# Router product of a two-layer flow backbone: the weights become the stationary operand, in two column tiles, and a second product turns the result back

## The reference, cut to what matters

```python
h2 = modulate(x, sh2, sc2)                       # (tokens, 1024)
f = hier_moe(h2.reshape(-1, d), w_router_group[layer], w_router_expert[layer], ...)

def hier_moe(t, w_router_group, w_router_expert, ...):
    p_group = jax.nn.softmax((t @ w_router_group).astype(jnp.float32), axis=-1)   # 4 groups
    grp = jnp.argmax(p_group, axis=-1).astype(jnp.int32)
    logits_e = jnp.einsum('td,dge->tge', t, w_router_expert)                      # 4 x 8 experts
    logits_sel = jnp.take_along_axis(logits_e, grp[:, None, None], axis=1)[:, 0]
    top_p, top_j = lax.top_k(jax.nn.softmax(logits_sel, axis=-1), TOP_K_FINE)     # 2 of 8
    ...
    return grouped_experts(...)
```

## Time and profile before

| | us |
|---|---|
| median of 3 runs | 2699.07 |
| the profiled execution | 2698.96 |
| its span, first to last instruction | 2697.1 |
| PE busy in it | 2331.0 (86%) |
| `attend` of layer 0, first scores to last logits | 376.6 to 684.2 |
| `attend` of layer 1, first scores to last logits | 1664.2 to 1916.0 |
| mean granted TensorE clock | 0.927 of full |

### The profile page before, as it was taken

How to read it: one execution, slowest core, us unless ns; L and a number is a source line. 1 busy time by engine, 2 the same in 40 slices (tenths; PEclk the granted TensorE clock), 3 DMA queues, 4 the chain that set the end, 5 groups by cost and what they waited for, 6 DMA issues and landing times. The chain is left out here.

```text
span 2697.1 us, 39484 instructions
## 1 busy us (share of the span) xinstructions
PE 2331.0 (86%) x15320; PEld 1642.8 (61%) x15320; DVE 863.8 (32%) x2138; ACT 430.6 (16%) x1058; POOL 500.2 (19%) x629
## 2 busy tenths in 40 slices
PE   4999879998299999999949987999389999999950
PEld 3999745654266666666629984556266666666630
DVE  1322435564610111101127665565711011111008
ACT  1010122221011111111101113222001111111112
POOL 0000013444011111111110011344011111111117
PEclk8999979998599999999979998999589999999985
DMA  9454430001397999999841113000289999999943
GB/s 356 147 185 153 155 109 11 22 22 41 136 369 294 392 400 389 387 399 394 327 160 65 47 41 130 20 24 16 83 349 391 391 384 395 386 386 381 371 190 128
DMA packets 130505, 608.65 MB, mean 226 GB/s; under 512 B 20608, under 2 KB 23680, under 8 KB 111984
## 3 DMA queue, kind: packets, MB, share of 16 engines
q1 hardware_dynamic: 112400, 569.61, 54.5%
q0 software_dynamic: 16864, 37.78, 3.7%
q10 hardware_dynamic: 1152, 0.03, 0.0%
HBM read 599.41 MB, written 42.04 MB: 238 GB/s over the span
## 5 line engine op out<-in xcount | busy, mean ns | idle before, releaser
L1874 PEld LDWEIGHTS gate_up<-room,w_gate_up 128*128 128x128 f32 x4608 | 521.1, 193 | 31.5 <-issue 31.5
L1874 PE MATMUL gate_up<-room,w_gate_up 128*128 128x128 f32 x4608 | 528.0, 277 | 3.1 <-DVE room L1781 3.1
L1883 PE MATMUL down<-w_down,room 128*128 128x512 f32 x576 | 256.8, 599 | 0.0
L1891 PE MATMUL gate_up_short<-w_gate_up,room 128*64 128x512 f32 x1152 | 255.1, 595 | 0.0
L1790 DVE TENSOR_TENSOR room<-room,gate_up 128x128 f32<-128x128 f32 x144 | 41.4, 288 | 597.8 <-ACT room L1809 597.8
L1891 PEld LDWEIGHTS gate_up_short<-w_gate_up,room 128*64 128x64 f32 x1152 | 79.5, 137 | 171.2 <-issue 171.2
L1883 PEld LDWEIGHTS down<-w_down,room 128*128 128x128 f32 x576 | 106.5, 190 | 123.0 <-issue 120.5
L1793 DVE TENSOR_TENSOR room<-room,gate_up_short 128x256 f32<-128x256 f32 x36 | 15.2, 421 | 495.1 <-ACT room L1815 495.1
L1501 POOL COPY rows_idx<-slot_token 128x1 int32 (+1 forms) x78 | 14.3, 183 | 789.9 <-PE rows_turned L1861 709.2
L1904 PE MATMUL down<-w_down,room 128*64 128x512 f32 x576 | 131.5, 598 | 11.9 <-ACT room L1817 11.9
L1325 PE MATMUL proj<-w_out,mixT 128*128 128x512 f32 x288 | 129.5, 592 | 0.0
(11 more groups left out here) (352 smaller groups left out, 3211.7 us busy)
## 6 DMA issues: line engine op xcount, KB each, us to landing
w_gate_up<-in_w_exp_gate SPq DMA_DIRECT2D x72, 2048.0 KB, 9.1
w_gate_up<-in_w_exp_up SPq DMA_DIRECT2D x72, 2048.0 KB, 13.8
w_down<-in_w_exp_down SPq DMA_DIRECT2D x72, 2048.0 KB
ada_w<-in_w_ada SPq DMA_DIRECT2D x48, 1024.0 KB, 7.0
h_rows<-h SPq DMA_DIRECT2D x18, 512.0 KB, 2.6
w_out<-in_w_out SPq DMA_DIRECT2D x2, 4096.0 KB, 13.9
w_in<-in_w_in SPq DMA_DIRECT2D x2, 3072.0 KB, 17.2
xn<-expert_rows SPq DMA_DIRECT2D x10, 512.0 KB, 4.0
```

Source lines behind the costliest of these rows:

```text
L1874: mm = nc.tensor.matmul(H[j % 2][:, o, :], wgu[0][:, o, k, j * P:(j + 1) * P], xT[0][:, k, :], start=k == 0, stop=k == KT - 1)
L1883: mm = nc.tensor.matmul(Y[:, h, :], hid[:, j, :], wd[0][:, j, h * 512:(h + 1) * 512], start=j == 0, stop=j == JT - 1)
L1891: mm = nc.tensor.matmul(Hs[c * HP:(c + 1) * HP, :, :], xT[1][:, k, :], wgu[1][:, :, k, c * 2 * P:(c + 1) * 2 * P], start=k == 0, stop=k == ...
```

## The change

The router's product is written the other way round. The weights, 128x36 for each slice of the channels, are stationary, and the turned rows move, 128 columns. The even slices are summed in PSUM partitions 0 to 35 (column tile 0), the odd ones in partitions 64 to 99 (column tile 1); each result has the logits in the partitions and the tokens in the columns. ScalarE copies the two to a 128x128 buffer `lt` in SBUF, whose other partitions hold zeros. One product with `lt` stationary and `fold` moving (two 36-column identities above one another) turns them back and adds them, into the second quarter of the same PSUM bank. ScalarE then copies 36 logits for each token, as before.

The second product, `router_rows(u)`, and ScalarE's last copy, `logits(u)`, are put into the next round: behind `scores(t, 0)` on PE, and ahead of the exponentials on ScalarE. `lt` and `fold` are set once for each layer by GpSimd, ahead of its first wait.

```diff
-        wr = sb("w_router", [P, KT, NR])
+        wr, fold, lt = sb("w_router", [P, KT, NR]), sb("fold", [P, NR]), sb("logitsT", [P, P])
+        r_set, r_full, lt_ready = sem("router_set"), sem("router_full"), sem("logitsT_ready")
 @block.gpsimd
+                nc.gpsimd.memset(lt[:, :], 0.0).then_inc(r_set, 1)
+                nc.gpsimd.tensor_tensor(fold[:, :], g.k[:, K_ID:K_ID + NR], g.k[:, K_ID + HD:K_ID + HD + NR], ALU.add).then_inc(r_set, 1)
                 add_one(0)
 @block.scalar
+                def logits(u):
+                    b, n = turn_of["router", u, 0, 0]
+                    act.wait_ge(T_full[b], n + 1)
+                    nc.scalar.activation(g.logits[:, u, :], T[b][:, 1, 0:NR], ACT.Copy).then_inc(T_read[b], 1)
                 for t in range(N + 2):
+                    if t >= 3:
+                        logits(t - 3)
                     if att(t):
...
                     if rtr(t):
                         b, n = turn_of["router", t - 2, 0, 0]
-                        act.wait_ge(T_full[b], n + 1)
-                        nc.scalar.activation(g.logits[:, t - 2, :], T[b][:, 0, 0:NR], ACT.Copy).then_inc(T_read[b], 1)
+                        act.wait_ge(r_full, t - 1)
+                        if t == 2:
+                            act.wait_ge(r_set, 2)
+                        for o in (0, HD):
+                            nc.scalar.activation(lt[o:o + NR, :], T[b][o:o + NR, 0, :], ACT.Copy).then_inc(lt_ready, 1)
+                logits(N - 1)
 @block.tensor, router(u)
                     if u == 0:
                         pe.wait_ge(router_in, 32)
+                        pe.wait_ge(r_set, 2)
...
                     for k in range(KT):
-                        mm = nc.tensor.matmul(T[b][:, 0, 0:NR], hT[:, k, :], wr[:, k, :], start=k == 0, stop=k == KT - 1)
-                    mm.then_inc(T_full[b], 1)
+                        o = k % 2 * HD
+                        mm = nc.tensor.matmul(T[b][o:o + NR, 0, :], wr[:, k, :], hT[:, k, :], start=k < 2, stop=k >= KT - 2)
+                    mm.then_inc(r_full, 1)
+                def router_rows(u):
+                    b, n = turn_of["router", u, 0, 0]
+                    pe.wait_ge(lt_ready, 2 * u + 2)
+                    nc.tensor.matmul(T[b][:, 1, 0:NR], lt[:, :], fold[:, :], start=True, stop=True).then_inc(T_full[b], 1)
                 for t in range(N + 2):
                     if att(t):
                         scores(t, 0)
+                    if t >= 3:
+                        router_rows(t - 3)
                     if prj(t):
...
                     if rtr(t):
                         router(t - 2)
+                router_rows(N - 1)
```

## The result

The changed kernel took 2682.11 us (median of 4 runs, 2681.02 to 2683.77) against 2699.37 for the kernel before (4 runs, 2698.83 to 2700.94): a ratio of 0.9938, interval 0.9922 to 0.9954, 17 us less. Two later comparisons gave 0.9946 (0.9932 to 0.9960) and 0.9944 (0.9930 to 0.9958). The forecast was 2688.0, 11 us less, with a range down to 2684.5: right in direction, too small in size.

A forecast was written before the change was run, and what follows sets the result against it. PE's own stream was taken to bound full rounds. Savings of 9.2 (full rounds), 0.7 and 0.25 (context rounds), 0 (round 7 of layer 1) and 0.8 (ends) sum to 11.0 us: 2698.96 to 2688.0 us, range 2684.5 to 2693.0.

The forecast's parts named there:

- The full rounds: Eleven rounds where scores follow the router: 1.08 us less there, 0.24 for turning back, net 0.84 each, 9.2 us in all.
- Pace: New router's passes in two column tiles in turn: 0.052 us a pass, against 0.119 for the old router.
- the turning back: Two added PE passes behind the scores in full rounds: 0.24 us more, bounds 0.1 and 0.6.
- the serial rival: Router's two column tiles don't run side by side: pace 0.104, 0.06 us gained a full round, 2702.5 us; chance 0.03.
- The cover of ScalarE: Full rounds: ScalarE's two copies end at 539.4, PE reaches the turning back at 540.3; no wait, 0.9 us in hand.
- The ends: Last round of each layer, serial: 3.67 us becomes 3.25, gain 0.4 a layer, 0.8 in all.
- round 7 of layer 1: Router to projection there: old 1.78 us, new 2.06 from 0.26 earlier; gain nil.
- the 0.6 named as a sign: About 0.6 us of PE idle time ahead of the turning back in round 10 of layer 0 and round 8 of layer 1.
- the way up to this router: Layer 1, first scores to the router of round 7: 4.5 us less.
- The context rounds: Rounds 8 and 9 of layer 0, where PE waits for DVE and the clock falls: gains of 0.7 and 0.25 us.
- the clock among the rivals: Clock falls in full rounds because the new router fills fewer columns: 2.25 us a fall, eleven give 2712.8 us; chance 0.04.

The follow-up runs named there:

- e7: Changed kernel with all 8 router slices in column tile 0, one sum and one ScalarE copy; ratio 0.9982 to the kernel before.
- e8: Changed kernel with the turning back and last copy right behind the router, in the same round; ratio 0.9982 to the kernel before.
- e12: Changed kernel with four old-router slices computed ahead of router 3 of layer 0 (overwritten), delaying all behind it; ratio 0.9949 to the kernel before.
- e3: Kernel before, with the new router in rounds 8 and 9 of layer 0 alone; ratio 0.9982 to the kernel before.
- e4: Changed kernel, with the old router in rounds 8 and 9 of layer 0 alone; ratio 0.9951 to the kernel before.
- e9: Kernel before, with 128 router columns moving instead of 36 in rounds 8 and 9 of layer 0 alone; ratio 0.9987 to the kernel before.
- e2: Kernel before, with the old router moving 128 columns of weights instead of 36 for each slice; 2694.93 us, ratio 0.9986.
- e6: Kernel before, with four router slices computed once more ahead of router 3 of layer 0 (overwritten), delaying all behind it; ratio 0.9999.
- e5: Kernel before, run again with no edit; ratio 0.9995.
- e10: Changed kernel, with the turning back behind the first half of the projection in round N; 2682.18 us, ratio 0.9936 to the kernel before.
- e1: Changed kernel, run again with no edit; 2683.95 us, ratio 0.9946 to the kernel before.

## Why the prediction was wrong

**The full rounds: right.** Pace 0.051 for 0.052 forecast, 1.08 us from the router's first load to the scores' for 1.09, 0.22 for the turning back for 0.24; the round shortened by 0.81, forecast 0.84. Eleven rounds make 8.9 us for 9.2. e7 shows that the mechanism is the one named, and in a full round the serial rival is what one tile does; its time was 2695 us and not the rival's 2702.5, since the context rounds and the unchanged part were shorter there too. The 0.60 between routers 7 and 8 of layer 0 is the same 0.81, less the earlier start of router 7.

**The cover of ScalarE: right.** No wait in full rounds, and e8 shows the price without the cover, 27.43 - 26.57 = 0.86 us. Of the rule of the Trainium skill (TensorE: Matmul & The Clock Gate, Part 3, The mechanism) that a weight load overlaps a product in flight only when its row group differs: the new router's loads span 0.88 and its products 1.04 us over one stretch, in two tiles of one row group. The trace disagrees with that rule here too. Loads and products share a stretch in e7's one tile as well (1.75 and 1.91 us), so it is the pace that tells the two forms apart.

**The ends, round 7 of layer 1: right.** The ends gave 0.37 a layer for 0.4. From the router of round 7 to the projection the new kernel takes 2.04 us, forecast 2.06; the old one took 1.78 and started 0.2 us later, so 0.1 us is lost. The idle time there was 0.93 us and not the 0.6 named as a sign, since it counts from the last load: from the end of the last product it is about 0.67. In layer 1 the way up to this router gave 3.8 us for 4.5; 0.2 of that are the five full rounds, the rest lies ahead of the router of round 2, a stretch that varies by 0.3 us between traces of one kernel.

**The context rounds: wrong.** This is the step that failed: I took the low stretch behind the wait as given, to be met by whatever work comes ("the stretch at 0.52 then covers work of the projection that ran ahead of it before at full clock"), and gave the two rounds 0.95 us. The traces of the changed kernel gave 5.2, 6.9, 6.9 and, in e12, 5.2 us: the low level lasted 13.7 us in the two rounds before and 3.4 or none after. e3 brings the gain with the new router in these rounds alone, e4 takes it away, and e9 gets most of it (4.9 us of the stage) with the old order and loads, by more moving columns. So what the router does behind the wait changes how long the clock stays low; the early falls show that it does not decide alone whether it falls. I had the clock among the rivals, but with the sign turned: that a narrower router would lose it. The products in fact moved more columns, 128 for 36, and the old router was the thin one.

**The unchanged parts: not forecast, and luck.** Of the 18.0 us between the first two traces, 14.4 are in the two stages and 3.6 in code that nobody changed: 3.8 between the stages and 1.1 behind them gained, 1.3 ahead of them lost. Over all fourteen traces the part between the stages takes 976.1 to 980.4 us, with one and the same code; the old kernel had 979.6 to 980.2 in its three, the changed one 976.4, 979.4, 978.9 and 980.1. The stages alone make 14.4 to 15.8 us (first, second and third trace of the changed kernel against the first of before), which is where the later ratios lie (14.5 to 15). The first comparison, 17 us, is the highest of the three and may hold some of this luck. With the context rounds sized rightly the forecast would have been 2684 to 2682.

**What stays open.** Why e2, e7, e8 and e9 all fell on 976 us in the unchanged part, though their shifts differ. They all have a low stretch of 3.4 us some 25 us ahead of the second `attend` where most of the others have 6.8, but so has e6, at 979.6; e2 and e9 also gain 1.1 to 1.3 us in the first 80 us behind the logits. The traces show where, not why. For the same reason the small gains in time of e2, e3, e7, e8 and e9, 3.5 to 5 us each, can't be put down to the context rounds by the times alone; e8 has such a gain with none in its stages. Each trace is one execution: those of e5, e6, e8 and e10 were the slowest of their runs, those of e1 and e9 the fastest. And open is what, beside the router, chooses between 3.4 us and none: e10 ruled out the gap behind router 9 as needed for it.

## What to carry to other kernels

Where TensorE has to wait a microsecond or two, look at the granted clock behind the wait and at what the first products behind it do. Here thin ones kept it low longer, and 6.8 us at the low level cost some 3 us (an estimate: 3.4 us cost 1.7, from the distances 25.67 and 23.97 of the changed kernel, and the next 3.4 us 1.5, from 27.65 before and 26.19 in e9). Turn small products round so that the wide operand moves, put them in two column tiles if the outputs fit 64 partitions, and put the step that needs another engine behind work that does not wait. When a saving rests on the clock, take several traces of both kernels before you size it: unchanged code moved by 4 us here.

## What the runs showed of the hardware that was not expected

A product widened from 36 to 128 moving columns, at the same pace of 0.12 us, shortened the low stretch of the first context round from 6.8 to 3.4 us; the kernel was faster by 0.13% (e9, 0.9978 to 0.9997), but its trace was also 3.8 us shorter in code that the edit does not touch. In all traces the low stretches of the context rounds were 3.4 or 6.8 us long and nothing between. Around a wait of 2.08 us the clock fell in 17 of 28 places, and in two of them a wait of 1.1 us more followed and the low stretch was 6.8 us with the new router too. And two column tiles in turn take an f32 pass of 128 moving columns from 0.109 to 0.051 us; with weights of 36 columns the pace is that of weights of 64 (0.052, L1296).
